# Two down projections of a two-block transformer step: from 48 weight blocks with plain products to three groups of seven products of sums, and the queue place of the second FFN's row-pair stores

## The reference

```
first  (f1):  x = x + g2 * ((silu(h @ w_gate) * (h @ w_up)) @ w_down)
second (f2):  u = causal_dwconv(h @ w_up, conv_w, conv_b); g, v = split(u)
              x = x + (silu(g) * v) @ w_down;   out = rmsnorm(x, final_norm_w)
...
FFN_HIDDEN = FFN_DIM = 2816, D_MODEL = 1024, SEQ = 1024, FFN_CONV = 3
```

## Time and profile before

| | |
|---|---|
| time, median of 3 runs | 2602.19 us (2599.89 to 2608.4) |
| the profiled execution | 2599.32 us, its span 2596.9 us |
| PE busy | 2523.5 us (97%), 12113 matmuls |
| DVE, POOL, ACT busy | 1454.1 us (56%), 1152.0 us (44%), 987.3 us (38%) |
| mean granted PE clock | 0.993 |
| down product of f1 | from 1158.5 to 1401.7 us |
| down product of f2 | from 2336.0 to 2578.4 us |
| DMA | 235.81 MB, mean 91 GB/s |

### The profile page before, as it was taken

One profiled execution on the slowest core, in us unless ns is written; L12 is line 12 of the kernel. 1 busy time (PEld: TensorE's weight loads), 2 busy tenths in 40 slices (PEclk: granted clock), 3 DMA queues, 4 the chain that ended last, 5 costly groups with the idle time before them and its releaser, 6 DMA issues.

```text
span 2596.9 us, 31637 instructions
## 1 busy us (share of the span) xinstructions
PE 2523.5 (97%) x12113; PEld 2030.2 (78%) x12113; DVE 1454.1 (56%) x1695; ACT 987.3 (38%) x1583; POOL 1152.0 (44%) x689
## 2 busy tenths in 40 slices
PE   7999999998999999999999999999998999999997
PEld 5778788887878888878886778777876888888886
DVE  5673288896186665654334111234198988876333
ACT  4652467876253323321113321233254444441113
POOL 0224222682575555555445211114465655556452
PEclk8999999999999999999999999999999999999999
DMA  7462010343312231234222111003212222234321
GB/s 294 134 210 63 23 54 14 84 106 119 106 49 89 106 106 65 82 130 149 87 81 98 41 33 41 30 28 115 97 41 82 73 90 90 73 128 176 104 79 65
DMA packets 71574, 235.81 MB, mean 91 GB/s; under 512 B 8946, under 2 KB 11122, under 8 KB 71299
## 3 DMA queue, kind: packets, MB, share of 16 engines
q1 hardware_dynamic: 71426, 233.80, 26.8%
HBM read 180.55 MB, written 39.85 MB: 85 GB/s over the span
## 4 chain that ended last, share of the span: by engine, by line
PE 86%; DVE 9%; ACT 2%; issue 2%; POOL 1%; DMA 1%; SPq 0%; DVEq 0%; ACTq 0%
PE S L871 18%; PE S L485 12%; PE S L486 11%; PE S L849 9%; PE S L853 9%; PE S L850 9%; PE MM L722 2%; PE S L722 2%; PE S L696 1%; DVE xt L1818 1%; PE MM L710 1%; PE S L697 1%; PE MM L488 1%; PE S L710 1%; PE S L504 1%
## 5 line engine op out<-in xcount | busy, mean ns | idle before, releaser
L2228 POOL TENSOR_TENSOR wbl<-rf,wbh 128x512 fp32r<-128x512 f32 (+1 forms) x352 | 512.7, 1462 | 454.2 <-ACT wbh L1264 454.0
L1264 ACT ACTIVATE wbh<-rf 128x512 fp32r<-128x512 f32 (+1 forms) x352 | 215.7, 619 | 666.2 <-PE S L871 355.5
L2105 POOL TENSOR_TENSOR wl<-raw,wh 128x1024 fp32r<-128x1024 f32 x59 | 148.8, 2523 | 553.9 <-ACT wh L1028 553.9
L849 PE MATMUL S<-th_t,wbh 128*128 128x512 f32 x640 | 252.9, 395 | 4.2 <-POOL wbl L2228 4.2
L853 PE MATMUL S<-tl_t,wbh 128*128 128x512 f32 x640 | 251.9, 394 | 0.0
L850 PE MATMUL S<-th_t,wbl 128*128 128x512 f32 x640 | 251.5, 393 | 0.0
L871 PE MATMUL S<-fl,wbh 128*128 128x512 f32 x704 | 219.4, 391 | 1.1 <-POOL fl L2252 1.1
L871 PE MATMUL S<-fh,wbh 128*128 128x512 f32 x704 | 220.3, 392 | 0.0
L871 PE MATMUL S<-fh,wbl 128*128 128x512 f32 x704 | 219.7, 391 | 0.0
L485 PE MATMUL S<-hh,wh 128*128 128x512 f32 (+1 forms) x456 | 194.7, 427 | 12.9 <-DVE gt L2034 3.1
L849 PE MATMUL S<-th_b,wbh 128*128 128x512 f32 x480 | 189.4, 395 | 4.5 <-DVE cu L1862 3.4
(11 more groups left out here) (352 smaller groups left out, 5461.0 us busy)
## 6 DMA issues: line engine op xcount, KB each, us to landing
ff<-hid SPq DMA_DIRECT2D x44, 512.0 KB, 6.0
rf<-in_w_d SPq DMA_DIRECT2D x80, 256.0 KB, 2.7
mr<-in_w_modT SPq DMA_DIRECT2D x32, 512.0 KB, 4.8
rf<-in_w_f1g SPq DMA_DIRECT2D x22, 512.0 KB, 3.6
rf<-in_w_f1u SPq DMA_DIRECT2D x22, 512.0 KB, 3.2
hid<-pr SPq DMA_DIRECT2D x22, 512.0 KB, 2.6
rf<-in_w_f2g SPq DMA_DIRECT2D x22, 512.0 KB, 5.3
rf<-in_w_f2u SPq DMA_DIRECT2D x22, 512.0 KB, 3.3
```

What stands on the lines that cost most here:

```text
L849: e.matmul(o, hi[:, k, :], th[part][:, k, :], start=k == 0, stop=False)
L1264: e.activation(flat(wbh[wslot(f, n)][:, :, :])[:, 0:x.shape[1]], x, ACT.Copy).then_inc(*w_hi.mark((f, n)))
L2105: e.tensor_tensor(l, raw[:, w % 3, 0:n], h.bitcast(F), ALU.subtract).then_inc(*w_lo.mark(w))
L2228: e.tensor_tensor(l, x, h.bitcast(F), ALU.subtract).then_inc(*w_lo.mark((f, n)))
```

## The change

*Down product.* The hidden dimension is cut into three groups of KT = 4, 4 and 3 pairs of tiles (8, 8 and 6 tiles, at `A0`). In each, the 8 output tiles are two halves of four, the hidden tiles two halves of KT, the tokens two halves of 512: 2x2 quarters of weights (a11, a12, a21, a22, `wq`) times 2x2 quarters of hidden rows (b11, ..., `xq_`), in seven products of sums in place of eight. A *unit* u = 7g + s is one product of one group, in the order 1, 2, 5, 3, 6, 7, 4 (`DOWN_ORDER`), and has four blocks i, each with 3 x KT matmuls. 21 units with 84 blocks take the place of 48 blocks.

For it DVE makes four sums of weights for each i and group (`weight_sum`, 16 a group), four sums of hidden quarters in two chunks each (`part_sum`, 8 a group), the low parts of five of seven hidden factors in two chunks (`part_x_lo`), and takes each block's PSUM away as 128x512 (`evict`). POOL makes the low parts of the other two (s = 0 and 3). ACT makes all high parts (`part_x_hi`) and `wbh`. A part common to several results, `u2`, is gathered in SBUF and added to three quarters at the end (`rest_u2`, at u = 18, three additions for each i). Tiles m = 0 to 3 of `xt` are finished with u = 18, tiles 4 to 7 with u = 19 and 20; their squares are taken in the last two units. At i = 0 of each unit PE waits for the high and low part of its hidden factor, chunk by chunk.

*Order in f2.* SP issues the loads of row group q = 4 ahead of the first store of a row pair, and so on for each later pair. ACT's `tap(2, 1)` and DVE's sums for q = 5 come at another place.

```diff
-DNG = [4, 2, 4, 4, 4, 4]
-GROUP = [_g for _g, _n in enumerate(DNG) for _ in range(_n)]
-DOWN = [(_g, _m) for _g in range(len(DNG)) for _m in range(8)]
+DOWN_ORDER = (1, 2, 5, 3, 6, 7, 4)
+KT = (4, 4, 3)
+A0 = (0, 8, 16)
+NU_ = 7 * len(KT)
+DOWN = [(_u, _i) for _u in range(NU_) for _i in range(4)]
+def chunks(u):
+    return ((0, 2), (2, KT[u // 7]))
...
+                for u, i in DOWN:
...
+                    for k in range(KT[g]):
+                        if i == 0:
+                            e.wait_ge(*a_th((f, "x", u, k // 2)))
+                        e.matmul(o, hi[:, k, :], ph[u % 3][:, k, :], start=fresh and k == 0, stop=False, skip_group_check=not fresh)
+                        e.matmul(o, lo[:, k, :], ph[u % 3][:, k, :], start=False, stop=False, skip_group_check=not fresh)
+                        if i == 0:
+                            e.wait_ge(*part_lo_done(f, u, k // 2))
+                        i_ = e.matmul(o, hi[:, k, :], pl[u % 3][:, k, :], start=False, stop=k == KT[g] - 1, skip_group_check=not fresh)
+                    i_.then_inc(*made.mark((f, n)))
...
-                    elif p == 4:
+                    elif p == 4 and q > 2:
                         tap(q, 1)
+                    elif p == 5 and q == 3:
+                        tap(2, 1)
...
+                for u, i in DOWN:
+                    s, g = u % 7, u // 7
+                    evict(u, i)
+                    if g == last and s == 4:
+                        rest_u2(u, i)
+                    if s == 0:
+                        if g == 0:
+                            weight_sum(g, 5, i)
+                            weight_sum(g, 7, i)
+                        weight_sum(g, 6, i)
+                    elif s == 1:
+                        weight_sum(g, 3, i)
+                    elif s == 6 and g < last:
+                        weight_sum(g + 1, 5, i)
+                        weight_sum(g + 1, 7, i)
+                    if i in (1, 2) and u + 1 < NU_ and (s + 1) % 7 not in (0, 3):
+                        part_x_lo(u + 1, i - 1)
+                    if s == 0 and g == 0 and i > 1:
+                        part_sum(g, 5, i - 2)
+                    elif s == 1 and i < 2:
+                        part_sum(g, 7, i)
+                    elif s == 2:
+                        part_sum(g, 6 if i < 2 else 4, i % 2)
+                    elif s == 6 and g < last and i % 2:
+                        part_sum(g + 1, 5, i // 2)
...
+                for u, i in DOWN:
+                    block_lo(f, down_at(u, i) + RING)
+                    if i in (1, 2) and u + 1 < NU_ and (u + 1) % 7 in (0, 3):
+                        part_x_lo(f, u + 1, i - 1)
+                    if u >= NU_ - 2:
+                        square(tag, i + 4 * (u - NU_ + 2))
...
-                    if q % 2 and q >= 3:
+                    if f == "f1" and q % 2 and q >= 3:
                         store_hidden(f, q - 2)
+                    if f == "f2" and q >= 4 and (q % 2 == 0 or q == last):
+                        store_hidden(f, q - 3 if q < last else last - 2)
...
+                load_weights(f, 0, 0)
+                load_quarter(f, 0, 0)
+                load_quarter(f, 0, 1)
+                load_weights(f, 0, 1)
...
+                load_quarter(f, 0, 2)
+                load_quarter(f, 0, 3)
+                load_weights(f, 0, 2)
+                load_weights(f, 0, 3)
```

More of the change, by code:

```diff
@@ L67, in last_load_use @@
         return FIRST_BLOCKS.index((r, 1))
[L68 to L70 removed]
+    return AT[r // 2, 4 if r % 2 else 3]
 class Signal:
@@ L191, with halves_of @@
 TT = {("nm", _k): _k % 3 for _k in range(8)}
+def halves_of(tag):
+    return (1, 0) if tag in ("nm", "out") else (0, 1)
 def res_event(res, m, final=True):
@@ L856, in ffn @@
                 SL.i = 2
[L858 to L868, removed]
-                        first, last = k == 0 and n_ == 0, k == DNG[g] - 1 and n_ == 2
-                        for r in halves:
-                            i = e.matmul(S[j][:, HALF[r]], wt[:, k, :], x[:, HALF[r]], start=first, stop=last)
-                    if k == DNG[g] - 1:
-                        i.then_inc(*made.mark((f, t) if 1 in halves else ("half", (f, t))))
@@ L875, in ffn, with bank_free @@
-                js = [SL.take(e, (f, down_at(0, m)), (d_res, (f, down_at(0, m)))) for m in range(2)]
-                for k in range(DNG[0]):
-                    for m in range(2):
-                        down(0, m, js[m], k)
-                for g, m in DOWN[2:]:
-                    t = down_at(g, m)
-                    final = g == len(DNG) - 1
-                    j = SL.take(e, (f, t), (d_res, res_event((f, t), m, final)))
-                    for halves in ((0,), (1,)) if final and m == 7 else ((0, 1),):
-                        for k in range(DNG[g]):
-                            down(g, m, j, k, halves)
+                def bank_free(u, i):
+                    p, g = DOWN_ORDER[u % 7], u // 7
+                    if p in (6, 7):
+                        return [(d_dn, (f, u - (3 if p == 6 else 2), i))]
+                    if g > 0:
+                        return [(d_dn, (f, u - (3 if p == 1 else 3), i))]
+                    x = i + (4 if p == 5 else 0)
+                    if x > 5:
+                        return ML.back[x - 6]
+                    return [y for t in range(NP - 6, NP) if t % 6 == x for y in given_up(f, t)]
@@ L1982, in ffn @@
                         q, p = PROD[t + RING + 1]
-                        if q >= 3:
+                        if q >= 3 and not (f == "f2" and (q, p) == (5, 1)):
                             weight_sums(f, q, {1: (5, 7), 6: (6,), 3: (3,)}.get(p, ()))
-                    if f == "f1" and t in (NP - 3, NP - 1):
-                        for a in range(2):
-                            hidden(f, dn, a + t - NP + 3)
                     if f == "f2" and t == NP - 1:
```

358 lines of the change are left out of this document (252 added, 106 removed).

## The result

| | before | changed |
|---|---|---|
| time, median | 2603.47 us (2599.89 to 2608.4, 4 runs) | 2655.82 us (2655.26 to 2658.58, 4 runs) |
| span of the profiled execution | 2596.9 us | 2653.0 us |
| mean granted PE clock | 0.993 | 0.980 |

The ratio is 1.0205, 95% interval 1.0192 to 1.0218: slower by 2%, where 0.7% was forecast. The sign was right, and the time lies 3.8 us above the range.

The account below looks back on a forecast made before the run. PE, busy 97% of the span, was taken as the bound. Terms -60.6 - 9 + 66 + 12 + 5 + 6 = +19.4 on 2599.3 gave 2618.7, plus 1: 2620 us, slower by 0.7%, range 2565 to 2652.

Parts of the forecast that it names:

- Stores, -9: Early f2: loads ahead of row-pair stores end a stall of DVE and PE; bounds 5 and 12.3, taken as -9 us.
- The sign, 150 to 165 matmuls from 1970 to 2010 us: Early f2: PE would do some 150 to 165 matmuls in this window in place of 122.
- Waits in the down products, +66: Both down products: PE waits for late low parts from DVE and POOL; +66 us, midway between 52 and 81.
- By hand: Walk through the units at the down products' starts: PE loses 10 us in f1 and 17 us in f2.
- the lower count: Both down products: exclusive DVE and POOL time nearly fills PE's; 22 us lost in f1, 30 in f2, 52 together.
- 76.3 of 77.1 us: Group 1 of a down product: mutually exclusive DVE and POOL work takes 76.3 of PE's 77.1 us.
- The walk: Down products unit by unit, DVE and POOL taking turns: 37 us lost in f1, 44 in f2, 81 as upper count.
- the sign for this mechanism: Down products: DVE's operations on 1024 columns would show medians above 1.6 us.
- the prediction's own test: Wrong if DVE's operations stay near 1.2 and 0.7 us, or PE's low-part waits come to under 40 us.
- Ends, +12, +5 and +6: Squares at the product ends: single-buffer chain in "out" +12 us, POOL's pace in "nm" +5, slow clock behind both +6.
- rival 4: Down products: upper count 81 us or more, slow clock after stalls (ten: +17); 2640 to 2665 us, chance 0.15.
- Rival 1: Down products: DVE and POOL collisions hardly reach PE; 2565 us, or 2583 to 2593 with intermediate collisions; chance 0.35.

Follow-up runs that it names:

- e1: The changed kernel with f2's row-pair stores, ACT's tap and DVE's sums for q = 5 back in their old places: 2656.82 us, ratio 1.0210.
- e8: The changed kernel with high and low parts for the next unit made ahead of the other work of the same block: 2597.24 us, ratio 0.9987.
- e5: The changed kernel with two buffers in place of one for the squares of "out": 2652.52 us, ratio 1.0194.
- e6: The changed kernel with unread matmuls filling PE's waits for x2 ahead of the sums of squares: 2650.02 us, ratio 1.0188.
- e7: The changed kernel with 296 unread matmuls filling PE's waits for low parts in the down products: 2643.82 us, ratio 1.0164.
- e11: e8 with u2's additions spread, earlier low parts and weight loads at the starts, two "out" square buffers, fillers before x2 waits: 2585.34 us, ratio 0.9937.

## Why the prediction was off

**What bounds the kernel.** Right: PE, and 264 matmuls are 60.6 us.

**Stores, -9.** Measured -3.8 for all between the two products, and e1 makes 1 to 2.4 of it the change's. The loads in front did give DVE its 6.4 us back (31.1 us busy of 40 before, 37.5 now), but the step from there to PE was wrong: PE's waits in this stretch came to 8.0 us before and 8.3 now. The sign, 150 to 165 matmuls from 1970 to 2010 us, seems to have come true (159), but changed is 22 us behind there, and that window holds work from before the stall; in the same work it is 129 for 122.

**Waits in the down products, +66.** Right in sum (67.8) and in place. By hand start of f1 10, f2 17; measured at u = 1 and 2: 6.15 + 0.33 + 1.04 + 2.96 = 10.5 and 12.1. But the reason for the lower count, "76.3 of 77.1 us" of exclusive work, "99% hardly will", was wrong: POOL idles for 96 us of the first product, and e8 does the same work with half the waits (14.3 + 16.1 + 4.0 us in the two products). The walk went through the programs in their order, with the low parts behind evictions and `wbl`, and so had the places right, but by itself it gave 81, or 13 too much: 27 for the two starts, 24 for the step to group 1 and 16 for that to group 2, where 22.6, 19.4 and 9.9 were measured. That 66 came out is in part luck: it is the mean of this and of 52, the count whose reason fell. That the cost hung on the order as much as on the amount, it didn't say. Nor did the sign for this mechanism come, medians above 1.6 us: the median was 1.22. By the prediction's own test ("near 1.2 and 0.7 us") the durations spoke against it and PE's waits for it.

**Ends, +12, +5 and +6.** Measured 12.25, 5.75 and 6.2; e5 and e6 show both mechanisms.

**The failed step** is the one that put the slow clock within the down products into rival 4 ("ten of them would be +17 on 81") and left it out of the sum. The waits in the sum were those of the forecast, 66; with them belonged the clock behind them. Measured beside the waits: 28.9 us, of which 19.9 slow clock and 9 the first matmuls behind each wait. 19.4 + 28.9 would have given 2649. With 17 for it, as rival 4 had it, the forecast would have been 2637. e7 shows that the clock isn't simply added: with most of it kept up, the time falls by 12 us, and 7.5 turn into waits.

**Rival 1** (the collisions hardly reach PE) was wrong for this order. With low parts first, e8 to e11, much of it holds: 2585 to 2597, where it had 2565, or 2583 to 2593 with intermediate collisions. **Rival 4** had the time (2640 to 2665) and the slow clock, but with waits of 81 us or more, where 67.8 were measured.

## What to carry to other kernels

When work is placed behind blocks that a ring of buffers ties to the bottleneck engine, ask what stands ahead of it that waits for this engine itself; a helper engine with 96 us of idle time was still late in every group here. Compare windows of the same work: a change moves everything behind it in time. Put what the next unit needs ahead of what the ring needs six blocks later, on all helper engines at once: half a mending gives a third. A sum of new waits of PE is not complete without the slow clock and the restart behind each, here 0.43 us per us of wait (28.9 to 67.8). Fillers in the waits gave back some 0.2 of it in e7.

## What was not expected of the hardware

The length of a wait doesn't tell whether the slow clock follows. Changed, windows that begin 0.4 us ahead of the end of a wait of 2.49 us and of one of 2.00 us (columns as above):

```profile
1258.00:1262.00 4.00, 3.57 (x9) 2.87 (x10) 3.79 (x5) 1.40 (x2) 2.75 (x3) 0.57 0.01 4
1286.00:1290.00 4.00, 3.64 (x16) 2.99 (x17) 3.45 (x5) 1.58 (x2) 1.62 (x1) 1.00 0.10 35
```

9 matmuls against 16. But a wait of 2.96 us (before 1194.96) was followed by no slow matmul in the next 7 us, one of 2.91 (before 2395.40) by fourteen; and behind one of 3.48 us (2505.66) came none. What decides is left open. Each wait has a first matmul that takes 0.33 to 0.35 us to the next in place of 0.23, or 0.47 to 0.59 where the clock is slow.
